# Layer 1's second MLP product with the weights moving and the tokens on the partitions, and the final norm along the rows

## The chip, the cores and the metric

The kernel runs on one core of a Trainium2 chip. The metric is the device time of one execution in microseconds, the median of several. Three runs of the kernel before gave 1903.33 us (1903.31 to 1904.78). TensorE (PE) multiplies into PSUM, VectorE (DVE) and ScalarE (ACT) read PSUM and work on SBUF, GpSimd (POOL) works on SBUF alone, and SyncE (SP) issues nearly all DMAs.

## What is computed

Two layers over 256 latent tokens and 256 context tokens, 1024 wide, in float32. After the attention-like branches each layer ends with the MLP below; layer 1's MLP and the final norm are for the latent tokens alone. The gate `g2` is a row of 1024 numbers, a sixth of `silu(c) @ w_ada[layer] + b_ada[layer]`.

```python
x = x + g1 * merge_branches(...)
x = x + g2 * squared_relu_mlp(modulate(rms_norm(x, norm2[layer]), sh2, sc2), w_up[layer], w_down[layer])
# squared_relu_mlp(h, w_up, w_down) = square(relu(h @ w_up)) @ w_down      w_up (1024, 4096), w_down (4096, 1024)
...
return rms_norm(x, final_norm)      # x * rsqrt(mean(x*x) + 1e-6) * final_norm
```

## The kernel before

**Layout.** `xT`, `hH`/`hL` and `yH`/`yL` are held transposed: features on the 128 partitions, tokens (context 0 to 255, latent 256 to 511) along the row, eight feature tiles `kt`. Each float32 operand is split in a high part (fp32r, written by ACT) and a rest (operand minus high part), and each product is made of three matmuls: high by high, high by rest, rest by high.

**Panels.** All large products are cut into 180 panels of 1024 x 256 weights, 1 MB each, numbered `p`. SP loads a panel into `raw[p % 4]` as soon as panel `p - 4` is done. ACT copies it to `wH[p % 3]` (`split`, two halves of 128x1024) and DVE subtracts into `wL[p % 4]`; ACT and DVE do this two panels ahead, at the beginning of their step for panel `p - 2`. PE (`run_panel`) holds a 128x128 tile of the weights and moves the tokens, 256 of them in layer 1 and 512 in layer 0, into `pp[p % 2]`, two banks per panel; the last matmul raises `panel_done`. Before its first matmul it waits for `slot_free[p % 2]` to reach `p // 2`: whoever reads the banks of a panel raises that semaphore afterwards. The order of all steps on all engines is the list `PLAN`, which `make_plan` writes out; each engine walks it and does its part of each step. `later` puts a step off until so many panels have been planned.

**The MLP.** Per quarter `g` of the 4096 hidden features four `up` panels and four `down` panels. After an `up` panel ACT takes relu into `y_tmp`, DVE squares, ACT writes `yH`, DVE `yL`. After a `down` panel DVE does two `scalar_tensor_tensor` (L1818), `xT += modT * pp`: so x is brought up to date in SBUF after every quarter. Layer 1 has 16 `down` panels, 152 to 155, 160 to 163, 168 to 171 and 176 to 179.

**Between `wo` and the MLP in layer 1.** `wo` (panels 144 to 147) updates `xT`; `squares` (ACT) and DVE sum x squared, `mean` (PE, L1058) adds across partitions, ACT takes the square root, DVE the reciprocal, `spread` (PE, L1068) spreads it along partitions, `apply` (DVE `n_t` and `n_h`, ACT `hH` L1482, POOL `hL`) makes the MLP's input. Around these stand `ada` steps (L1096): `c` times a piece of `w_ada`, four pieces for layer 1's `g2` (group 11). `adarow` (DVE) copies their sums to SBUF, `adaturn` (PE, L1123) turns them, `modulation` (DVE) adds `b_ada` and writes `modT`. The order is `ada ada squares mean ada spread ada apply`, then the first halves of two `up` panels.

**The end.** After each of the last `down` panels: `squares`, and `final_turn`, where ACT multiplies `xT` by `final_norm` into `f_x` and PE transposes it (L1079, four 128x128) into a `pc` bank. After the last panel: `final_mean` over the partitions, square root, reciprocal, and `final`: ACT scales the first 512 columns (L1455) and DVE the other 512 (L2133) from PSUM into `f_out`, and SP stores the two halves of the tokens (L945).

Of the kernel before, what the change touches and what calls it, by code (L numbers as in the profile page):

```python
# [180 lines left out]
def make_plan():  # L181
# [20 lines left out]
    def later(at, k, **kw):  # L202

        owed.append((at, lambda: step(k, 0, **kw)))
        owed.sort(key=lambda q: q[0])

    def row_turn(at, g):

        for wait, k in ((1, "adarow"), (2, "adaturn"), (2, "modulation")):
            later(at + wait, k, g=g)  # L210
# [48 lines left out]
    for l in range(DEPTH):  # L259
# [134 lines left out]
        spread_apply(l, 2, 1)  # L394
# [12 lines left out]
        step("squares", l + 1, n=1, j=NC - 1)  # L407
        if more:
            step("mean", l + 1, n=1)
            ada()  # L410
        else:
            step("final_mean", DEPTH, n=1)
            step("final_turn", DEPTH, n=1, j=NC - 1)
    step("final", DEPTH)
# [5 lines left out]
    group_use = {}  # L420
# [16 lines left out]
    for st in plan:  # L437
# [8 lines left out]
        elif k == "final_turn":  # L446

            if st["j"] % 2 == 0:
                for tt in range(LAT // P):
                    use(st, tt, 2 * (st["j"] // 2) + tt)  # L450
                turn_use = st["u"]
            else:
                st["u"] = turn_use
# [63 lines left out]
        elif k == "final":  # L517
            for j in (0, 2):
                q = next(q for q in plan if q["k"] == "final_turn" and q["j"] == j)
                for tt in range(LAT // P):  # L520
                    st["u"][j // 2, tt] = q["u"][tt]
# [11 lines left out]
def trunk(nc, x, c, ctx_in, c_ctx, w_ada, b_ada, norm1, norm2, w_in, gate_b, mnorm, qnorm, knorm, conv_w,  # L533
          w_pm, w_pa, w_pc, w_out, w_up, w_down, fnorm, consts, out):
    ctx = ExitStack()
    with ctx:
# [73 lines left out]
        f_x = at("f_x", [P, 2, LAT], F32, T + 30720)  # L610
# [7 lines left out]
        n_sd, n_rs = small[:, 4:8], small[:, 8:12]  # L618
        q_sd, q_rs = small[:, 16:24], small[:, 24:32]
        pars = [at(f"pars{i}", [P, P if i < 2 else 24], F32, o + 512 * i) for i in range(3)]; o += 1120  # L620
# [55 lines left out]
        fx_ready = sem("final_x_ready")  # L676
        fx_half = sem("final_x_first_tile")
        fa_ready = sem("final_first_half_ready")
        fx_used = sem("final_x_turned")
# [70 lines left out]

        def panel_source(st):
            kind, l, c, b = st["kind"], st["l"], st["c"], st["b"]
            if kind in COL:
# [35 lines left out]
        for st in PLAN:  # L789
# [14 lines left out]
            elif k == "panel" and st["kind"] in ("wo", "down"):  # L804
# [63 lines left out]
        def _(sp):  # L868
# [32 lines left out]
            def load_panel(p):  # L901
                sp.dma_start(raw[:, p % RAW, :, :], panel_source(PANELS[p])).then_inc(s_raw[p % RAW], 16)
# [4 lines left out]
            sp.dma_start(par_rows[2][16:24, :], fnorm.rearrange("(r q) -> r q", q=P)).then_inc(s_small, 16)  # L907
# [9 lines left out]
            for st in PLAN:  # L917
                if st["k"] == "panel" and (st["kind"], st["c"]) == ("mk", 0):
# [7 lines left out]
                    for g in range(2):  # L926
                        for dr in range(2):
                            sp.dma_start(gb[dr * 4:dr * 4 + 4, g:g + 1],
                                         gate_b[l, dr, g].rearrange("(h a) -> h a", a=1)).then_inc(s_wg, 16)
                if st["k"] == "pairload":  # L930
# [18 lines left out]
        def _(pe):  # L949
# [11 lines left out]

            def run_panel(st, kts=slice(0, KT)):
# [4 lines left out]
                hs_, ls_ = p % HIGH, p % RAW  # L967

# [49 lines left out]
            for st in PLAN:  # L1018
# [5 lines left out]
                elif k == "start":  # L1024
                    pe.wait_ge(s_small, 64)
                    filled(pe.transpose(claim(u["par2"])[:, 0:24], par_rows[2][0:24, :], ident[0:24, 0:24]), u["par2"])
# [19 lines left out]
                elif k in ("mean", "final_mean"):  # L1046

                    if k == "mean":
                        b = claim(u["ss"])
                    else:  # L1050
                        pe.wait_ge(slot_free[NPANELS % 2], NPANELS // 2)
                        b = pp[:, NPANELS % 2, 0, :]
# [6 lines left out]
                    if k == "mean":  # L1059
                        filled(last, u["ss"])  # L1060
                    else:
                        last.then_inc(panel_done, 1)
# [8 lines left out]
                elif k == "final_turn":  # L1071
                    j = st["j"]
                    pe.wait_ge(fx_half, j + 1)
                    pe.wait_ge(fx_ready, j + 1)
                    for tt in range(LAT // P):
                        b = claim(u[tt]) if j % 2 == 0 else pc[:, u[tt][0], :]
                        for i in range(2):
                            at_ = (j % 2 * 2 + i) * P
                            last = pe.transpose(b[:, at_:at_ + P], f_x[:, i, tt * P:(tt + 1) * P], ident)  # L1079
                        if j % 2:  # L1080
                            filled(last, u[tt])
                        elif tt:
                            last.then_inc(fx_used, 1)
# [204 lines left out]
        def _(act):  # L1288
# [25 lines left out]
            for st in PLAN:  # L1314
# [107 lines left out]
                elif k in ("mean", "final_mean"):  # L1422
# [4 lines left out]
                    if k == "mean":  # L1427
                        b = bank(act, u["ss"])
                    else:
                        act.wait_ge(panel_done, NPANELS + 1)  # L1430
                        b = pp[:, NPANELS % 2, 0, :]
                    act.activation(n_sd[:, t0:TT], b[:, t0:TT], ACT.Sqrt, bias=eps).then_inc(sd_ready, 1)
                elif k == "final_turn":

                    j = st["j"]
                    act.wait_ge(x_ready, x_needed(st))
                    if j:
                        if j % 2:
                            act.wait_ge(fx_used, j // 2 + 1)
                        else:  # L1440
                            for tt in range(LAT // P):
                                act.wait_ge(full[u0[tt][0]], u0[tt][1] + 1)
                    u0 = u
                    for i in range(2):
                        g = 16 + 2 * j + i
                        last = act.activation(f_x[:, i, :], xT[:, 2 * j + i, CTX:TOK], ACT.Copy, scale=pars[2][:, g:g + 1])
                        if i == 0:
                            last.then_inc(fx_half, 1)
                    last.then_inc(fx_ready, 1)
                elif k == "final":  # L1450

                    act.wait_ge(nrs_ready, n_norm)
                    for tt in range(LAT // P):
                        b = bank(act, u[0, tt])
                        act.activation(f_out[:, tt, 0:D // 2], b[:, :], ACT.Copy,  # L1455
                                       scale=n_rs[:, CTX // P + tt:CTX // P + tt + 1]).then_inc(fa_ready, 1)
# [218 lines left out]
        def _(dve):  # L1675
# [25 lines left out]
            for st in PLAN:  # L1701
                k, l, u = st["k"], st["l"], st["u"]
                if k == "start":
                    up = u["par2"]
                    freed(dve.tensor_copy(pars[2][:, :], bank(dve, up)[:, 0:24]), up)
# [35 lines left out]
                elif k == "panel":  # L1741
# [61 lines left out]
                    elif kind == "up":  # L1803
# [6 lines left out]
                                          ALU.subtract).then_inc(y_ready, 1)  # L1810
# [364 lines left out]
```

## Time and profile before

| | |
|---|---|
| median of 3 runs | 1903.33 us |
| the profiled execution | 1904.54 us |
| its span, first to last instruction | 1902.5 us |
| PE matmul busy | 1854.5 us (97%) |
| PE weight load busy | 1598.2 us (84%) |
| DVE, ACT, POOL busy | 1062.7, 690.4, 158.2 us |
| mean granted TensorE clock | 0.989 of full |
| DMA | 244.56 MB, mean 129 GB/s |

In a timeline a row gives the start, the time taken, the engine, the line of the kernel, the operation, output <- inputs, sizes and count; in brackets how long the engine had been idle and for whom. Consecutive matmuls overlap, so what one costs is the distance between two starts, not its own duration. A row of windows gives the stretch, its length, the busy time (and count) of PE, then, where asked for all engines, of PE weight loads, DVE, ACT and POOL, then the granted clock, the DMA share and GB/s. A row of groups gives line, engine, operation, operands, form, count, busy us and mean ns.

### The profile page before, as it was taken

What the parts mean: (1) busy time and instruction counts of PE and PEld (TensorE: products, weight loads), DVE (VectorE), ACT (ScalarE), POOL (GpSimd) and SP (SyncE); (2) the same over time, 40 slices, a digit from 0 to 9 for tenths busy, and PEclk for the clock granted to TensorE, in tenths of its full rate; (3) what the DMA queues carried; (4) which work ended last, traced back from release to release, by engine and by line L of the source; (5) the groups of instructions that cost most, each with busy time, mean ns of one, the idle gap of its engine ahead of it and who ended that gap; (6) DMA issues with size and microseconds to landing.
All of it is one profiled execution on the core that took longest, in us unless ns stands there. A gap on an engine that the chain in (4) does not pass through costs nothing.

```text
span 1902.5 us, 26175 instructions
## 1 busy us (share of the span) xinstructions
PE 1854.5 (97%) x10845; PEld 1598.2 (84%) x10845; DVE 1062.7 (56%) x1562; ACT 690.4 (36%) x946; POOL 158.2 (8%) x158
## 2 busy tenths in 40 slices
PE   6999999999999999989999999899999999999998
PEld 4797788888888888867888888699998899989997
DVE  5535643545556666467565554644646656566664
ACT  3423543333222222343232223333544434444443
POOL 2101100001110111220000000200100110120000
PEclk9999999999999999999999999999999999999999
DMA  9221122211443453624443525232242365555552
GB/s 322 69 87 45 45 89 67 67 61 51 133 147 119 151 191 101 221 95 149 133 136 130 199 89 180 66 110 70 65 132 89 111 222 181 190 184 180 188 187 89
DMA packets 226293, 244.56 MB, mean 129 GB/s; under 512 B 5796, under 2 KB 210944, under 8 KB 226176
## 3 DMA queue, kind: packets, MB, share of 16 engines
q1 hardware_dynamic: 225872, 242.80, 39.8%
q8 instruction: 86, 1.41, 0.3%
q14 instruction: 31, 0.25, 0.0%
q10 hardware_dynamic: 304, 0.10, 0.0%
HBM read 241.84 MB, written 1.05 MB: 128 GB/s over the span
## 4 chain that ended last, share of the span: by engine, by line
PE 91%; DVE 4%; ACT 1%; SPq 1%; issue 1%; DMA 1%; POOL 0%; DVEq 0%; ACTq 0%
PE pp L1004 20%; PE pp L1008 20%; PE pp L1005 19%; PE pp L1013 5%; PE pp L1011 5%; PE pp L1012 5%; PE pc L1193 3%; PE pp L986 2%; PE pp L987 2%; PE pp L988 2%; PE pc L1245 1%; PE pc L1283 1%; SPq L884 1%; PE pc L1260 1%; DMA raw<-in_w_in 1%
## 5 line engine op out<-in xcount | busy, mean ns | idle before, releaser
L1004 PE MATMUL pp<-hH,wH 128*128 128x512 f32 (+1 forms) x1760 | 590.9, 346 | 4.4 <-ACT hH L1482 4.4
L1005 PE MATMUL pp<-hH,wL 128*128 128x512 f32 (+1 forms) x1760 | 581.3, 341 | 0.0
L1697 DVE TENSOR_TENSOR wL<-raw,wH 128x1024 fp32r<-128x1024 f32 x358 | 448.6, 1294 | 203.3 <-ACT wH L1297 200.1
L1297 ACT ACTIVATE wH<-raw 128x1024 fp32r<-128x1024 f32 x360 | 360.4, 1050 | 356.1 <-PE pp L1013 173.9
L1008 PE MATMUL pp<-hL,wH 128*128 128x512 f32 (+1 forms) x1760 | 456.4, 341 | 2.6 <-POOL hL L1635 1.9
L1004 PEld LDWEIGHTS pp<-hH,wH 128*128 128x128 f32 x1760 | 335.2, 190 | 50.7 <-issue 14.8
L1005 PEld LDWEIGHTS pp<-hH,wL 128*128 128x128 f32 x1760 | 335.1, 190 | 37.6 <-issue 1.7
L1008 PEld LDWEIGHTS pp<-hL,wH 128*128 128x128 f32 x1760 | 304.3, 190 | 43.8 <-POOL hL L1635 6.8
L1011 PE MATMUL pp<-yH,wH 128*128 128x512 f32 (+1 forms) x448 | 150.8, 337 | 0.0
L1012 PE MATMUL pp<-yL,wH 128*128 128x512 f32 (+1 forms) x448 | 150.6, 336 | 0.0
L1013 PE MATMUL pp<-yH,wL 128*128 128x512 f32 (+1 forms) x448 | 150.6, 336 | 0.0
L1004 PE MATMUL pp<-yH,wH 128*128 128x512 f32 (+1 forms) x448 | 149.3, 344 | 0.0
L1005 PE MATMUL pp<-yH,wL 128*128 128x512 f32 (+1 forms) x448 | 146.0, 337 | 0.0
L1008 PE MATMUL pp<-yL,wH 128*128 128x512 f32 (+1 forms) x448 | 114.1, 336 | 0.0
L1818 DVE SCALAR_TENSOR_TENSOR xT<-pp,modT,xT 128x256 f32<-128x256 f32 x120 | 50.7, 478 | 98.9 <-PE pp L1013 98.8
L1870 DVE SCALAR_TENSOR_TENSOR acc<-pair_W,c_wide,acc 128x512 f32<-128x512 f32 x126 | 102.2, 848 | 3.8 <-DVE xT L1818 1.2
L1004 PEld LDWEIGHTS pp<-yH,wH 128*128 128x128 f32 x448 | 85.3, 190 | 10.9 <-issue 2.4
L1005 PEld LDWEIGHTS pp<-yH,wL 128*128 128x128 f32 x448 | 85.2, 190 | 9.4 <-issue 0.7
L1013 PEld LDWEIGHTS pp<-yH,wL 128*128 128x128 f32 x448 | 85.2, 190 | 8.7
L986 PE MATMUL pp<-wH,hH 128*128 128x256 f32 x320 | 92.5, 289 | 0.0
L1012 PEld LDWEIGHTS pp<-yL,wH 128*128 128x128 f32 x448 | 85.1, 190 | 8.7
L1011 PEld LDWEIGHTS pp<-yH,wH 128*128 128x128 f32 x448 | 85.1, 190 | 8.8
(235 smaller groups left out, 2076.6 us busy)
## 6 DMA issues: line engine op xcount, KB each, us to landing
raw<-in_w_in SPq DMA_DIRECT2D x84, 1024.0 KB, 5.2
raw<-in_w_up SPq DMA_DIRECT2D x32, 1024.0 KB, 5.6
raw<-in_w_down SPq DMA_DIRECT2D x32, 1024.0 KB, 5.2
pair_W<-in_w_ada SPq DMA_DIRECT2D x10, 2048.0 KB, 7.9
ada_Y<-in_w_ada SPq DMA_DIRECT2D x10, 1024.0 KB, 11.9
ada_H<-in_w_ada SPq DMA_DIRECT2D x8, 1024.0 KB, 11.9
raw<-in_w_proj_m SPq DMA_DIRECT2D x8, 1024.0 KB, 5.3
raw<-in_w_proj_a SPq DMA_DIRECT2D x8, 1024.0 KB, 5.4
```

Source lines behind the costliest of these rows:

```text
L986: pe.matmul(dst, hi[:, kt, ts_], wH[:, hs_, kt, :], start=kt == 0, stop=False)
L1004: pe.matmul(dsts[b], wh[b], hi[:, kt, ts_], start=first, stop=False)
L1005: pe.matmul(dsts[b], wl[b], hi[:, kt, ts_], start=False, stop=False)
L1008: last = pe.matmul(dsts[b], wh[b], lo[:, kt, ts_], start=False, stop=end)
L1011: pe.matmul(dsts[b], wh[b], hi[:, kt, ts_], start=first, stop=False)
L1012: pe.matmul(dsts[b], wh[b], lo[:, kt, ts_], start=False, stop=False)
L1013: last = pe.matmul(dsts[b], wl[b], hi[:, kt, ts_], start=False, stop=end)
L1193: last = pe.matmul(b[:, 0:MV + 1], EP[:, d, off:off + P], vaug[:, s, h, :], start=i == 0, stop=i == len(terms) - 1)
L1297: act.activation(wH[:, p % HIGH, a:a + KH, :], raw[:, p % RAW, a:a + KH, :], ACT.Copy).then_inc(wH_ready, 1)
L1697: dve.tensor_tensor(wL[:, p % RAW, ks, :], raw[:, p % RAW, ks, :], wH[:, p % HIGH, ks, :].bitcast(F32), ALU.subtract).then_inc(wL_ready, 1)
L1818: i = dve.scalar_tensor_tensor(out=xT[:, kt, hs], in0=pp[:, slot, b, hs], scalar=modT[:, l, g + kt, v:v + 1], in1=xT[:, kt, hs], op0=ALU.m ...
L1870: i = dve.scalar_tensor_tensor(out=acc[:, v, :], in0=src[:, kt, :], scalar=c2[:, kt, v:v + 1], in1=acc[:, v, :], op0=ALU.mult, op1=ALU.add)
```

## The change

- A `down` panel of layer 1 (`natural`) is now 512 rows by 512 columns of `w_down`: still 1 MB, column half `ch = c // 2`, row half `kh = c % 2`; `wide` views the same buffers as four tiles of 128x512. In `run_sums` PE holds a 128x128 tile of `yH` or `yL` (128 tokens) and moves 512 weight columns: 4 row tiles x 2 token halves x 3 = 24 matmuls a panel. They add into the four `pc` banks (column half x token half) from the first quarter to the last; `pp` is not used and x not updated between. The last panel of a column half (177 and 179) goes token half by token half.
- L1818 falls away for these 16 panels. In its place DVE waits for `panel_done` and raises `slot_free`, except after the last two panels. Panels 177 and 179 raise `full` of their banks and not `panel_done`.
- New `turn_nat`, twice: PE transposes eight 128x128 tiles of `xT` into two banks, ACT copies them to `x_nat` (two of 128x512). Once between `mean` and `spread`, in the place of an `ada`, which moves behind `spread`; once after the first `up` panel.
- New `gate_nat` in the place of `adaturn` and `modulation` of group 11: four 128x256 matmuls with float32 operands spread the gate row over all partitions in two banks; DVE adds `b_ada` (two of 128x512) into `g_nat`. SP loads `b_ada`'s row and `final_norm`, each repeated on 128 partitions, 512 KB each, ahead of panel 150.
- `squares`, `final_turn`, `final_mean` and `final` at the end are replaced by four `tail` steps (column half, token half), planned after panels 177 and 179.
- `final_norm` is no longer loaded by SP at the start (L907).

```diff
@@ make_plan
-        ada()
-        if l == 0:
+        if more:
+            ada()
+            spread_apply(l, 2, 1)
 ...
+        else:
+            step("turn_nat", l, half=0)
+            spread_apply(l, 2, 2)
+            later(count["panel"] + 1, "turn_nat", l, half=1)
 ...
-                if g == FF // D - 1 and c:
+                if more and g == FF // D - 1 and c:
                     step("squares", l + 1, n=1, j=c - 1)
-                    if not more:
-                        step("final_turn", DEPTH, n=1, j=c - 1)
+                if not more and g == FF // D - 1 and c % 2:
+                    for tt in range(LAT // P):
+                        step("tail", l, ch=c // 2, tt=tt)
@@ PE
+            def run_sums(st):
+                p, l, b_, u = st["p"], st["l"], st["b"], st["u"]
+                ch, kh = divmod(st["c"], 2)
+                first, end = (b_, kh) == (0, 0), (b_, kh) == (FF // D - 1, 1)
+                order = [(k_, tt) for k_ in range(KH) for tt in range(LAT // P)]
+                if end:
+                    order = [(k_, tt) for tt in range(LAT // P) for k_ in range(KH)]
+                for n, (k_, tt) in enumerate(order):
 ...
+                    pe.matmul(banks[tt], yH[:, kt, ts_], wh[:, k_, :], start=first and k_ == 0, stop=False)
+                    pe.matmul(banks[tt], yH[:, kt, ts_], wl[:, k_, :], start=False, stop=False)
+                    last = pe.matmul(banks[tt], yL[:, kt, ts_], wh[:, k_, :], start=False, stop=end and k_ == KH - 1)
+                    if end and k_ == KH - 1:
+                        filled(last, u[tt])
+                if not end:
+                    last.then_inc(panel_done, 1)
             def run_panel(st, kts=slice(0, KT)):
                 if p >= 2 and kts.start == 0:
                     pe.wait_ge(slot_free[slot], p // 2)
+                if natural(st):
+                    run_sums(st)
+                    return
@@ DVE
+                    elif natural(st):
+                        if p + 2 < NPANELS:
+                            dve.wait_ge(panel_done, p + 1)
+                            dve.sem_inc(slot_free[slot], 1)
+                elif k == "tail":
+                    if n == 0:
+                        dve.wait_ge(xn_ready, 2)
+                    dve.tensor_tensor(f_t[:, :], b, g_nat[:, cs], ALU.mult).then_inc(ft_ready, 1)
+                    dve.wait_ge(ft_ready, 2 * n + 1)
+                    v = x_nat[:, tt, cs]
+                    dve.tensor_tensor(v, v, f_t[:, :], ALU.add).then_inc(ft_ready, 1)
+                    dve.wait_ge(ft_ready, 2 * n + 2)
+                    i = dve.tensor_tensor(f_out[:, tt, cs], v, fn_nat[:, cs], ALU.mult)
+                    if ch == 0:
+                        i.then_inc(fn_ready, 1)
+                    else:
+                        start_link(i)
+                        dve.wait_ge(fd_ready, tt + 1)
+                        dve.reciprocal(n_rs[:, tt:tt + 1], n_sd[:, tt:tt + 1]).then_inc(fr_ready, 1)
+                        dve.wait_ge(dchain, count[0])
+                        dve.wait_ge(fr_ready, tt + 1)
+                        dve.tensor_scalar(f_out[:, tt, cs], f_out[:, tt, cs], n_rs[:, tt:tt + 1], None,
                                           ALU.mult).then_inc(f_ready, 1)
@@ ACT, tail
+                    act.wait_ge(ft_ready, 2 * n + 2)
+                    if n:
+                        act.wait_ge(fs_ready, n)
+                    act.activation(f_sq[:, :], x_nat[:, tt, ch * (D // 2):(ch + 1) * (D // 2)], ACT.Square,
+                                   accum_out=f_ss[:, n:n + 1]).then_inc(fs_ready, 1)
+                    act.wait_ge(fs_ready, n + 1)
+                    if ch == 0:
+                        act.activation(f_b[:, tt:tt + 1], f_ss[:, n:n + 1], ACT.Identity, scale=1.0 / D,
+                                       bias=eps).then_inc(fb_ready, 1)
                     else:
+                        act.wait_ge(fb_ready, tt + 1)
+                        act.activation(n_sd[:, tt:tt + 1], f_ss[:, n:n + 1], ACT.Sqrt, scale=1.0 / D,
+                                       bias=f_b[:, tt:tt + 1]).then_inc(fd_ready, 1)
+                        act.wait_ge(fr_ready, tt + 1)
+                        act.wait_ge(fn_ready, tt + 1)
+                        act.activation(f_out[:, tt, 0:D // 2], f_out[:, tt, 0:D // 2], ACT.Copy,
+                                       scale=n_rs[:, tt:tt + 1]).then_inc(fa_ready, 1)
```

## Rows read from the trace of the kernel before

**Rows 1.** Page, part 4: the chain that ended last, shares of the span.
```profile
PE 91%; DVE 4%; ACT 1%; SPq 1%; issue 1%; DMA 1%; POOL 0%; DVEq 0%; ACTq 0%
```

**Rows 2.** Windows, all engines: 50 us inside layer 1's MLP.
```profile
1750.00:1800.00 50.00, 50.00 (x419) 50.00 (x418) 29.35 (x36) 21.95 (x26) 0.00 (x0) 1.00 0.57 182
```

**Rows 3.** Timeline of PE: first matmul of panels 176 and 177, 256 columns moving.
```profile
1867.47 0.28 PE L1004 MATMUL pp<-yH,wH 128*128 128x256 f32 x1
...
1873.23 0.28 PE L1004 MATMUL pp<-yH,wH 128*128 128x256 f32 x1
```

**Rows 4.** Timeline of PE in layer 0's MLP, 512 columns moving, ten matmuls apart.
```profile
900.05 0.39 PE L1005 MATMUL pp<-yH,wL 128*128 128x512 f32 x1
...
902.32 0.39 PE L1005 MATMUL pp<-yH,wL 128*128 128x512 f32 x1
```

**Rows 5.** Windows, all engines: an `mv` panel, tokens held and weights moving.
```profile
1300.00:1304.00 4.00, 4.00 (x35) 4.00 (x35) 0.00 (x0) 0.00 (x0) 0.00 (x0) 1.00 0.00 0
```

**Rows 6.** Timeline of PE: `final_turn` between panels 177 and 178.
```profile
1878.99 0.60 PE L1079 MATMUL pc<-con,f_x 128*128 128x128 f32 x4
...
1879.55 0.28 PE L1005 MATMUL pp<-yH,wL 128*128 128x256 f32 x1
```

**Rows 7.** Timeline of PE from layer 1's second `mean` to the first `up` matmul.
```profile
1699.99 0.58 PE L1058 MATMUL pc<-small,n_sum 128*128 128x1 f32 x4 [1.32 <-DVE n_sum L1902]
1700.50 1.07 PE L1096 MATMUL pc<-ada_Y,c_wide 128*32 128x256 f32 x16
1701.50 0.86 PE L1068 MATMUL pc<-con,small 128*128 128x128 f32 x4
1702.29 1.94 PE L1096 MATMUL pc<-ada_Y,c_wide 128*32 128x256 f32 x16
1704.15 0.58 PE L1004 MATMUL pp<-hH,wH 128*128 128x256 f32 x1
```

**Rows 8.** Windows of PE alone: granted clock in that stretch.
```profile
1702.00:1703.00 1.00, 1.00 (x10) 0.50 0.00 0
```

**Rows 9.** Timeline of DVE and of ACT in that stretch.
```profile
1701.01 0.17 DVE L1908 RECIPROCAL small<-small 128x2 f32<-128x2 f32 x1 [1.17 <-ACT small L1432]
...
1702.98 1.32 ACT L1482 ACTIVATE hH<-n_t,modT,gain 128x256 fp32r<-128x256 f32 x2 [2.11 <-DVE n_t L1926]
```

**Rows 10.** Timeline of PE: `adaturn`, and four float32 products of 128x256 (eight records).
```profile
1717.17 0.61 PE L1123 MATMUL pc<-con,ada_rows 128*128 128x8 f32 x4 [0.27 <-DVE ada_rows L1728]
...
1444.68 1.89 PE L1283 MATMUL pc<-prT,v_a 128*128 128x256 f32 x8
```

**Rows 11.** Timeline, all engines, from the last panel's end.
```profile
1891.36 0.60 PE L1079 MATMUL pc<-con,f_x 128*128 128x128 f32 x4
...
1891.57 0.87 DVE L1818 SCALAR_TENSOR_TENSOR xT<-pp,modT,xT 128x256 f32<-128x256 f32 x2 [4.12 <-PE pp L1013]
...
1894.70 0.58 PE L1058 MATMUL pp<-small,n_sum 128*128 128x1 f32 x4 [2.74 <-DVE n_sum L1902]
...
1898.77 0.36 SPq L945 DMA_DIRECT2D out<-f_out  x1
```

**Rows 12.** Groups by form: the operations nearest to those of `tail`.
```profile
L1805 DVE TENSOR_TENSOR y_tmp<-y_tmp 128x512 f32<-128x512 f32 x16 | 11.1, 693 | 19.9 <-ACT y_tmp L1394 19.9
...
L2115 DVE TENSOR_SCALAR pr<-pr,ars 128x512 f32<-128x512 f32 x32 | 14.1, 483 | 0.7 <-DVE ars L2111 0.2
...
L1523 ACT ACTIVATION_READ_ACCUMULATOR junk<-hM 128x1 f32 x24 | 4.9, 203 | 0.0
L1527 ACT ACTIVATE mrs<-mss,small 128x2 f32<-128x2 f32 x4 | 1.2, 296 | 0.0
L1421 ACT ACTIVATE n_sq<-xT 128x512 f32<-128x512 f32 x6 | 3.7, 620 | 8.0 <-DVE xT L1818 8.0
L1455 ACT ACTIVATE f_out<-pc,small 128x512 f32<-128x512 f32 x2 | 1.3, 677 | 0.0
```

**Rows 13.** Timeline of SP's queue at the start.
```profile
1.96 0.29 SPq L907 DMA_DIRECT2D par_rows<-in_final_norm  x1
```

More of the change, by code:

```diff
@@ L406, in make_plan @@
             ada(2)
[L407 to L408 removed]
+            step("squares", l + 1, n=1, j=NC - 1)
             step("mean", l + 1, n=1)
             ada()
[L411 to L414, printed above, removed]
     assert count["ada"] == len(ADA) and not owed
@@ L445, in make_plan @@
             st["u"] = spread_use
-        elif k == "final_turn":
-            if st["j"] % 2 == 0:
+        elif k == "turn_nat":
+            for tt in range(LAT // P):
+                use(st, tt, 2 * tt)
+        elif k == "gate_nat":
+            for i in range(2):
+                use(st, i, 1 + 2 * i)
+        elif k == "panel" and st["kind"] == "down" and st["l"] == DEPTH - 1:
+            ch, kh = divmod(st["c"], 2)
+            if (st["b"], kh) == (0, 0):
                 for tt in range(LAT // P):
-                    use(st, tt, 2 * (st["j"] // 2) + tt)
-                turn_use = st["u"]
-            else:
-                st["u"] = turn_use
+                    use(st, tt, 2 * ch + tt)
+                sum_use[ch] = st["u"]
+            else:
+                st["u"] = sum_use[ch]
+        elif k == "tail":
+            st["u"] = {0: sum_use[st["ch"]][st["tt"]]}
         elif k == "turn_x":
@@ L803, in trunk @@
                 h_no[l, "m", st["j"]] = n_h_; n_h_ += 1
-            elif k == "panel" and st["kind"] in ("wo", "down"):
+            elif k == "panel" and st["kind"] in ("wo", "down") and not natural(st):
                 x_no[l, st["kind"], st["b"], st["c"]] = n_x; n_x += 1
@@ L1058, in _ @@
                         last = pe.matmul(b[:, tt:tt + 1], n_sum[:, tt * P:(tt + 1) * P], mean_d, start=True, stop=True)
[L1059 to L1062, printed above, removed]
+                    filled(last, u["ss"])
                 elif k == "spread":
@@ L1070, in _ @@
                     filled(last, u["rs"])
[L1071 to L1074, printed above, removed]
+                elif k == "turn_nat":
+                    half = st["half"]
+                    pe.wait_ge(x_ready, x_no[l, "wo", 0, 2 * half + 1] + 1)
                     for tt in range(LAT // P):
[L1076 to L1083, printed above, removed]
+                        b = claim(u[tt])
+                        for i in range(KH):
+                            last = pe.transpose(b[:, i * P:(i + 1) * P],
+                                                xT[:, half * KH + i, CTX + tt * P:CTX + (tt + 1) * P], ident)
+                        filled(last, u[tt])
+                elif k == "gate_nat":
+                    for i in range(2):
+                        b = claim(u[i])
+                        for c in range(2):
+                            r = 2 * (2 * i + c)
+                            last = pe.matmul(b[:, c * PC:(c + 1) * PC], row_sum[:, r:r + 1].to_broadcast([P, P]),
+                                             ada_rows[:, st["g"] % 2, :], start=True, stop=True)
+                        filled(last, u[i])
                 elif k == "ada":
@@ L1426, in _ @@
                         act.wait_ge(s_const, 4)
-                    if k == "mean":
-                        b = bank(act, u["ss"])
-                    else:
[L1430 to L1456, printed above, removed]
```

117 lines of the change are left out of this document (83 added, 34 removed).

## Prediction

> **What bounds the kernel now.** I read the chain of work that ended last first: 91% of the span is TensorE [rows 1]. Then windows of 50 us through layer 1's MLP: PE is busy in all 50, at full clock, DVE in 29.35 and ACT in 21.95, DMA at 0.57 [rows 2]. So in that stage time goes only with what PE issues; DVE, ACT and DMA work there is covered, and DVE's L1818, which the change removes 16 times, is worth nothing by itself. Then the two places where the MLP's neighbours set the time: from the second `mean` to the first `up` matmul [rows 7 to 9], and the end, from the last panel's end at 1891.36 to 1902.5, 11.1 us in which PE is nearly idle [rows 11]. The sum below is made on the profiled execution (1904.54, span 1902.5); the median of the runs is 1903.33, 1.2 lower, and I take the saving off the median.
>
> **1. The 16 panels: -5.1.** Panel 176 takes from 1867.47 to 1873.23, 5.76 us for 48 matmuls of 256 columns, 0.120 each [rows 3]. Ten matmuls of 512 columns take 2.27 us, 0.227 each [rows 4]. 24 of these are 5.44: 0.32 less per panel, 16 x 0.32 = 5.1. What goes is a part that each matmul costs however many columns it moves: 2 x 0.120 - 0.227 = 0.013. The bound from above is the same row. From below, the row of 512 has tokens moving and weights held, here it is the other way; the nearest row of that kind is the `mv` panel, 256 wide, 35 matmuls in 4 us, no slower than rows 3 [rows 5]. I keep 5.1, 4.6 at the least. The Trainium skill ("TensorE: Matmul & The Clock Gate", section Back-to-back issue gap) gives an issue gap of N/2.4 + 2.5 ns for a single stream. By that page 256 columns cost 0.109 and 512 cost 0.216, and the saving would be an estimated 16 x (48 x 0.1092 - 24 x 0.2158) = 1.0 us and not 5.1. Rows 3 and 4 disagree with it by 11 ns per matmul at both widths, and I go by the rows.
>
> Waits that could take the place: a `down` panel now needs only half of `yH` at first, so that is easier than before. Splits, loads (1 MB each as before) and the `slot_free` signals run two and more panels ahead, with 20 us of 50 free on DVE [rows 2]. None of it ends last, with one exception (part 4).
>
> **2. `final_turn` out of the panels: -0.9.** From the first of its four transposes to the second matmul of panel 178 are 0.56 us, and one matmul issue is 0.12: 0.44 [rows 6, 3]. Two of the four lie between panels: 0.9. The other two lie in the end, part 5.
>
> **3. Ahead of the MLP: +1.9.** (a) The `ada` between `mean` and `spread` took 1.00 (1700.50 to 1701.50) at full clock; eight transposes take its place, 0.09 each, 0.7 in all (a quarter of 0.44 less the slower first matmul) [rows 6, 7]. `spread` then starts when the reciprocal is there (1701.01 + 0.17), at 1701.25, 0.25 earlier, and with it `apply`. ACT's two copies (0.6 each, like L1421's 0.62) end near 1702.3 and `hH` is due at 1702.98 [rows 9, 12]: covered by 0.4, and if not, 0.4 is what it costs. But two `ada` stand behind `spread`, in the stretch where the clock is half (0.50) and one takes 1.86 (1702.29 to 1704.15) [rows 7, 8]. The first `up` matmul starts some 1.2 later than 1704.15. The matmuls it displaces would have run at half clock and behind `apply`, so most comes back; I take +0.2, between -0.2 and +1.2. (b) The second `turn_nat` has no idle time to go into: eight transposes, +0.7. Its two copies add 1.2 to ACT, covered by ACT's free half [rows 2]; without that cover, up to 1.2. (c) `adaturn` costs 0.27 of waiting and 0.46 of issue (0.61 less the 0.16 by which a matmul outlasts its issue). `gate_nat` is four float32 products of 128x256 in eight records, like L1283's, 1.89 - 0.16 = 1.73 [rows 10]. The wait is gone since PE comes 0.7 later: +1.0. The two adds on DVE (0.69 each, [rows 12]) have 20 us of 50 to go into. The two repeated rows, 1 MB, are issued by SP between panels 149 and 150, far ahead of use, at a DMA share of about 0.6: nothing. Sum 0.2 + 0.7 + 1.0 = 1.9, bounds +1.3 and +3.3.
>
> **4. A stall of PE ahead of the last panel: +0.4.** Panel 177 is the last of its banks and does not raise `panel_done`. DVE's step for it waits until `panel_done` is 178, which comes only when panel 178 is done, and only then raises `slot_free`, for which PE waits ahead of panel 179. The nearest row of such a hand-over is 0.21 from the last issue of PE to DVE's start (0.16 of it the matmul's own end) [rows 11]; back the same without the 0.16, with the semaphore step 0.4. Bounds 0.2 and 1.0. Queued behind that wait on DVE are the two `tail` steps of the first column half: meant to run beside panel 178, they begin when it ends.
>
> **5. The end, with the stall: -2.5.** Counted from the end of panel 178. Before: 0.44 + 5.76 + 11.13 = 17.3. After: DVE begins at 0.3 with tail 0 and 1, six operations of 0.69 and a hand-over of 0.05: to 4.75. The bank for tail 2 is full at 0.4 + 2.7 + 0.2 = 3.3, so DVE is late by 1.4. Tail 2: two operations to 6.2; ACT square 0.62, reading its sum 0.20, square root 0.30 with hand-overs to 7.4; reciprocal 0.2, scaling 0.48, to 8.1 [rows 12]. Tail 3's bank is full at 0.4 + 5.44 + 0.2 = 6.0, DVE comes at 8.1: 9.6, 10.8, reciprocal 11.0, ACT's 512 columns 0.68, 11.7. The last store before went from 1898.77 to the end at 1902.5, 3.7 [rows 11], beside the first one; alone on the DMA I count 3.1. 14.8 in all, 2.5 less. The bound from above is full overlap of all hand-overs and a store of 2.6, 3.4 less; from below 1.5 less. Of the 2.5 the stall of part 4 has already taken its 0.4.
>
> **6. The start: -0.2.** One DMA issue less on SP (0.29, from 1.96) ahead of the load of x, for which PE waits [rows 13]. 0 to 0.3.
>
> **Sum.** The last panel and the second `final_turn` lie inside part 5, so parts 1 and 2 count 15 panels (4.8) and one `final_turn` (0.4): -4.8 - 0.4 + 1.9 - 2.5 - 0.2 = **-6.0**. The profiled execution would go from 1904.5 to 1898.5 (span 1896.5), the median from 1903.3 to **1897.3**.
>
> **Rivals.**
> A. *The half clock comes more often.* The clock fell after an idle stretch of 1.32 us and the work at 1702 to 1705 ran at 0.50 [rows 7, 8]. The stall of part 4 and the new pauses could bring more such stretches: one like that from 1702 to 1705 costs half its length, 1.5, two cost 3.0. Against it: waits of 0.27 [rows 10] were followed by no fall. Two of them: 1903.3 - 6.0 + 3.0 = 1900.3.
> B. *The width gives nothing here*: with the weight buffers moving a matmul of 512 columns costs as much as two of 256, 0.240. Then 4.8 of the 6.0 are gone: 1902.1. Rows 4 speak against it, though with the roles the other way. By the rule of the Trainium skill's page cited in part 1 the gain of the width would be an estimated 1.0 and the time 1901.2.
> C. *The load of the held operand shows*, slower. PE now holds tokens and the weight load (busy like PE itself in rows 2) has to hide behind a matmul that reads rows of 512 from the weight buffers. If each of 384 matmuls cost 0.050 more (0.277), that is +19: 1916.5. It decides from 6.0/384 = 0.016 (a distance of 0.243) on, and is slower by over 0.2% from (6.0 + 3.8)/384 = 0.026 (0.253) on. Against it: rows 4, where PE's load hides, and rows 5, the same roles.
> D. *The tail goes better*: DVE's wait of part 4 does not bind and tails 0 and 1 run beside panel 178. Tail 2 then starts with its bank at 2.9 and takes DVE the same 3.35, tail 3 starts at 6.3 and not at 8.1: 1903.3 - 6.0 - 1.8 = 1895.5. The code speaks against it.
>
> **Chances.** Forecast 0.70, A 0.14, B 0.05, C 0.04, D 0.07. The ends of the terms, all at once, give savings from 4.3 + 0.4 - 3.3 + 1.5 = 2.9 (15/16 of 4.6, no gain at the start) to 4.8 + 0.4 - 1.3 + 3.4 + 0.3 = 7.6, so 1895.7 to 1900.4; to take in A and D the range is 1894.9 to 1900.8. B and C stay outside. What a measurement of this kernel can tell from no change is about 0.2%, 3.8 us. The forecast and D are faster by more than that; A (3.0) and B (1.2) are within it; C is slower. Faster 0.77, same 0.19, slower 0.04.
>
> **What would show it.** Right: matmuls of `run_sums` 0.227 apart and panels 5.44 apart; no idle time of PE inside the MLP but about 0.4 ahead of panel 179, put down to DVE; `gate_nat` 1.7; DVE busy without a gap from the end of panel 178 until tail 2's square root; about 9 us from PE's last matmul to the end. Wrong: a distance above 0.23, a clock under 1.00 in the MLP, PE waiting for `wL` or for DVE behind `gate_nat`, or the tails of the first column half beside panel 178.

## The result and the profile after

| | before | after |
|---|---|---|
| median | 1903.61 us (1903.31 to 1904.78, 4 runs) | 1891.97 us (1890.20 to 1894.92, 4 runs) |
| ratio | | 0.9939, 95% interval 0.9922 to 0.9957 |
| profiled execution | 1904.54 us | 1894.92 us |
| its span | 1902.5 us | 1893.2 us |

The saving is 11.6 us, where the forecast was 6.0 and the range ended at 1894.9. Run again beside other kernels (e5_change_again) the ratio was 0.9931. In e5_change_again one execution of six took 9583.39 us, and no trace shows why; it is in the median given for that run and not in its ratio. The profiled execution after is the slowest of its four, so its trace understates the saving (9.3 between the spans); the account below says by what.

Windows of all engines over 50 us of layer 1's MLP after, to be read against [rows 2]:

```profile
1750.00:1800.00 50.00, 50.00 (x333) 46.23 (x332) 26.79 (x26) 22.55 (x26) 0.00 (x0) 1.00 0.60 190
```

PE is still busy throughout at full clock; DVE has 26 operations in place of 36, and as forecast that is worth nothing by itself.

The timeline of PE at the end of panel 178 and the start of 179 (lines 1014 to 1016 are `run_sums`):

```profile
1878.07 0.39 PE L1016 MATMUL pc<-wH,yL 128*128 128x512 f32 x1
1878.30 0.39 PE L1014 MATMUL pc<-wH,yH 128*128 128x512 f32 x1
1878.53 0.39 PE L1015 MATMUL pc<-wL,yH 128*128 128x512 f32 x1
1878.75 0.39 PE L1016 MATMUL pc<-wH,yL 128*128 128x512 f32 x1
1879.26 0.50 PE L1014 MATMUL pc<-wH,yH 128*128 128x512 f32 x1
1879.59 0.39 PE L1015 MATMUL pc<-wL,yH 128*128 128x512 f32 x1
```

Starts are 0.227 apart, and 0.51 between the panels: the stall is 0.28. The next start is 0.33 later and not 0.227, and the panel's last matmul (1884.62) comes 0.43 later than it would have at 0.227 throughout.

Then the view I should have compared first, PE's longest waits. The columns are the waiting line, what ended the wait, total us, times, longest us. Before:

```profile
PE pc L1058 <- DVE n_sum L1902: 11.9, 4, 4.2
PE pc L1123 <- DVE ada_rows L1728: 5.1, 4, 3.4
```

After (L1118 is `mean`, L1186 `adaturn`):

```profile
PE pc L1118 <- DVE n_sum L1973: 11.9, 4, 4.3
PE pc L1186 <- DVE ada_rows L1795: 1.1, 2, 0.5
```

The second pair differs by 4.0 us, and only 0.27 of that is the wait of [rows 10]. One wait of 3.45 in layer 0 is nearly all the rest. Timeline of DVE and PE there, before:

```profile
855.62 1.23 DVE L1809 TENSOR_TENSOR yL<-y_tmp,yH 128x1024 fp32r<-128x1024 f32 x1 [1.13 <-ACT yH L1302]
...
856.76 0.88 DVE L1868 TENSOR_SCALAR acc<-pair_G,c_wide 128x512 f32<-128x512 f32 x2
...
857.68 2.86 DVE L1870 SCALAR_TENSOR_TENSOR acc<-pair_G,c_wide,acc 128x512 f32<-128x512 f32 x4
860.58 0.42 DVE L1728 COPY ada_rows<-pc 128x256 f32<-128x256 f32 x1
...
861.05 0.61 PE L1123 MATMUL pc<-con,ada_rows 128*128 128x8 f32 x4 [3.45 <-DVE ada_rows L1728]
```

After:

```profile
855.48 1.23 DVE L1876 TENSOR_TENSOR yL<-y_tmp,yH 128x1024 fp32r<-128x1024 f32 x1 [1.13 <-ACT yH L1365]
...
856.62 0.42 DVE L1795 COPY ada_rows<-pc 128x256 f32<-128x256 f32 x1
...
856.96 0.88 DVE L1939 TENSOR_SCALAR acc<-pair_G,c_wide 128x512 f32<-128x512 f32 x2
...
857.32 0.51 PE L1186 MATMUL pc<-con,ada_rows 128*128 128x8 f32 x4
```

The short copy for which PE waits now stands ahead of the six long operations of `weighted` and not behind them. The wait of 3.45 is gone. And so is what followed it. Windows with the granted clock as third number from the end, before and then after:

```profile
863.00:864.00 1.00, 1.00 (x3) 0.75 (x3) 1.00 (x2) 0.00 (x0) 0.00 (x0) 0.50 0.00 0
```

```profile
863.00:864.00 1.00, 1.00 (x6) 0.81 (x5) 1.00 (x2) 0.00 (x0) 0.00 (x0) 1.00 0.00 0
```

Why the order changed stands in the first hunk of the diff. In layer 0 `spread_apply(l, 2, 1)` used to come behind the block that queues the `weighted` steps with `later`; now it comes ahead of it. The `ada` inside it is the fourth piece of layer 0's own `g2`, so it queues `adarow` for the next panel. Both fall due at the same panel, the sort that takes them out keeps equals in the order in which they were queued, and so `adarow` now wins.

**An account by one row.** DVE's subtraction into `wL` of a given panel is the same work in both kernels, so its start is a clock that both traces share. Before, for panels 49, 97, 145, 154 and 178:

```profile
701.98 1.22 DVE L1697 TENSOR_TENSOR wL<-raw,wH 128x1024 fp32r<-128x1024 f32 x1
...
1267.28 1.22 DVE L1697 TENSOR_TENSOR wL<-raw,wH 128x1024 fp32r<-128x1024 f32 x1
...
1670.35 1.70 DVE L1697 TENSOR_TENSOR wL<-raw,wH 128x1024 fp32r<-128x1024 f32 x1 [4.91 <-ACT wH L1297]
...
1732.40 1.23 DVE L1697 TENSOR_TENSOR wL<-raw,wH 128x1024 fp32r<-128x1024 f32 x1 [0.25 <-ACT wH L1297]
...
1870.64 2.36 DVE L1697 TENSOR_TENSOR wL<-raw,wH 128x1024 fp32r<-128x1024 f32 x2 [0.25 <-ACT wH L1297]
```

After:

```profile
701.80 2.36 DVE L1764 TENSOR_TENSOR wL<-raw,wH 128x1024 fp32r<-128x1024 f32 x2
...
1261.92 1.23 DVE L1764 TENSOR_TENSOR wL<-raw,wH 128x1024 fp32r<-128x1024 f32 x1
...
1668.03 1.70 DVE L1764 TENSOR_TENSOR wL<-raw,wH 128x1024 fp32r<-128x1024 f32 x1 [4.91 <-ACT wH L1360]
...
1731.34 2.36 DVE L1764 TENSOR_TENSOR wL<-raw,wH 128x1024 fp32r<-128x1024 f32 x2 [0.26 <-ACT wH L1360]
...
1865.81 2.36 DVE L1764 TENSOR_TENSOR wL<-raw,wH 128x1024 fp32r<-128x1024 f32 x2 [0.26 <-ACT wH L1360]
```

| stretch | after less before | what it is |
|---|---|---|
| start to 701.98 | -0.18 | the start, and what varies from run to run there |
| to 1267.28 | -5.18 | the order in layer 0 |
| to 1670.35 | +3.04 | more work at half clock, no edit |
| to 1732.40 | +1.26 | ahead of and at the head of layer 1's MLP |
| to 1870.64 | -3.77 | 12 panels of 512 columns |
| to the span's end | -4.47 | 3 more such panels, a `final_turn`, the end |
| sum | -9.30 | 1902.5 to 1893.2 |

The third line is not the change's doing. Windows of PE alone, where both kernels do the same work, before and then after:

```profile
1292.00:1300.00 8.00, 8.00 (x56) 0.79 0.19 66
```

```profile
1286.00:1294.00 8.00, 8.00 (x43) 0.57 0.28 98
```

The half-clock stretch there is twice as long after (clock 0.57 against 0.79 of 8 us), and another one at 1429 likewise. In e5_change_again, the same kernel, that last place ran at full clock and the span was 1888.7. So single profiles of one kernel differ by several us in this way. The first stretch varies too: the row at 701.80 after stands at 700.12 in e5_change_again, so its -0.18 says nothing. The other stretches repeat: 560.12 after and 560.40 in e5_change_again for the second, 63.31 and 63.33 for the fourth, 134.47 and 134.46 for the fifth. With the third line taken out, the two traces differ by 12.3 us.

### The profile page after: what moved, and what is told of

It reads as the page before. It is cut to its first block, busy times and chain, and to the rows that moved or that the text cites. A ratio compares the mean times of both kernels' runs of the same rounds, so it can differ in the third digit from the quotient of the medians.

```text
span 1893.2 us, 25365 instructions
## 1 busy us (share of the span) xinstructions
PE 1851.3 (98%) x10461; PEld 1580.6 (83%) x10461; DVE 1052.4 (56%) x1537; ACT 691.0 (37%) x948; POOL 158.3 (8%) x158
## 4 chain that ended last, share of the span: by engine, by line
PE 91%; DVE 4%; SPq 1%; ACT 1%; issue 1%; DMA 1%; POOL 0%; DVEq 0%; ACTq 0%; POOLq 0%
PE pp L1068 19%; PE pp L1072 19%; PE pp L1069 19%; PE pp L1077 4%; PE pp L1076 4%; PE pp L1075 4%; PE pc L1256 3%; PE pp L1050 2%; PE pp L1051 2%; PE pp L1052 2%; PE pc L1308 2%; PE pc L1346 1%; PE pc L1016 1%; PE pc L1014 1%; PE pc L1015 1%; SPq L914 1%
## 5 line engine op out<-in xcount | busy, mean ns | idle before, releaser
L1068 PEld LDWEIGHTS pp<-hH,wH 128*128 128x128 f32 x1760 | 333.7, 190 | 47.6 <-issue 11.6
L1068 PE MATMUL pp<-yH,wH 128*128 128x512 f32 (+1 forms) x320 | 115.3, 367 | 0.0
L1075 PE MATMUL pp<-yH,wH 128*128 128x512 f32 (+1 forms) x320 | 114.3, 357 | 0.0
L1077 PE MATMUL pp<-yH,wL 128*128 128x512 f32 (+1 forms) x320 | 114.3, 357 | 0.0
L1076 PE MATMUL pp<-yL,wH 128*128 128x512 f32 (+1 forms) x320 | 114.3, 357 | 0.0
L1069 PE MATMUL pp<-yH,wL 128*128 128x512 f32 (+1 forms) x320 | 112.3, 358 | 0.0
L1051 PE MATMUL pp<-wL,hH 128*128 128x256 f32 x320 | 92.6, 290 | 0.0
L1052 PE MATMUL pp<-wH,hL 128*128 128x256 f32 x320 | 92.5, 289 | 0.0
L1072 PE MATMUL pp<-yL,wH 128*128 128x512 f32 (+1 forms) x320 | 88.4, 357 | 0.0
L1365 ACT ACTIVATE yH<-y_tmp 128x1024 fp32r<-128x1024 f32 (+1 forms) x48 | 40.6, 847 | 96.5 <-DVE y_tmp L1862 44.8
L1889 DVE SCALAR_TENSOR_TENSOR xT<-pp,modT,xT 128x256 f32<-128x256 f32 x88 | 36.7, 477 | 62.2 <-PE pp L1077 62.2
L1068 PEld LDWEIGHTS pp<-yH,wH 128*128 128x128 f32 x320 | 60.5, 189 | 10.9 <-issue 2.4
L1069 PEld LDWEIGHTS pp<-yH,wL 128*128 128x128 f32 x320 | 60.5, 189 | 9.3 <-issue 0.7
## 6 DMA issues: line engine op xcount, KB each, us to landing
ada_H<-in_w_ada SPq DMA_DIRECT2D x8, 1024.0 KB, 11.6
```

The costliest lines, as they stand in the source:

```text
L1051: pe.matmul(dst, hi[:, kt, ts_], wL[:, ls_, kt, :], start=False, stop=False)
L1052: last = pe.matmul(dst, lo[:, kt, ts_], wH[:, hs_, kt, :], start=False, stop=kt == KT - 1)
L1068: pe.matmul(dsts[b], wh[b], hi[:, kt, ts_], start=first, stop=False)
L1069: pe.matmul(dsts[b], wl[b], hi[:, kt, ts_], start=False, stop=False)
L1072: last = pe.matmul(dsts[b], wh[b], lo[:, kt, ts_], start=False, stop=end)
L1075: pe.matmul(dsts[b], wh[b], hi[:, kt, ts_], start=first, stop=False)
```

## The experiments

Each kernel was run beside the one before: 1904.31 us (9 runs) for the first four, 1905.21 (11) for the next two, 1904.97 (9) for the last two.

### The order in layer 0 alone, and the rest alone

Theory: the missing term is the order in layer 0, worth 5.1 or more. Rival: the terms that I did cost are larger than I said. e1_order is the kernel before with nothing but

```diff
         if l == 0:
+            spread_apply(l, 2, 1)
 ...
-        spread_apply(l, 2, 1)
+        else:
+            spread_apply(l, 2, 1)
```

and e2_old_order is the changed kernel with that call moved back behind the block of pairs.

```diff
-            spread_apply(l, 2, 1)
 ...  for i in range(NC): later(at + 31, "adaload", a=FILL_N1 + i)
+            spread_apply(l, 2, 1)
```

> The kernel before with one edit of the plan: in layer 0, spread_apply stands ahead of the list of weight pairs, as in the changed kernel. Theory (order): adarow, due with the same panel as the first weighted step, now comes first on DVE; PE's wait of 3.45 us for ada_rows near 860 us goes, and with it the half-clock stretch of 3.4 us that followed it (1.7 us): 5.1 us faster, about 1898.5, and no wait of PE for ada_rows over 1 us in the MLP of layer 0. Rival (sizes): the order is worth nothing and the panels, the end or the start were worth more than I said: about 1903.6, no change.

> The changed kernel with the old order of that place. Theory (order): the wait of 3.4 us comes back and the time goes from 1892.0 to about 1897, which is what was forecast for the change without this part (1897.3). Rival (sizes): it stays at 1892.

Measured: e1_order 1898.53 (1897.22 to 1900.58, 5 runs), ratio 0.9967 (0.9955 to 0.998), so -5.8. e2_old_order 1897.73 (1895.7 to 1899.24, 5 runs), ratio 0.9961 (0.9947 to 0.9975), so -6.6. Together -12.4. In e2_old_order the wait is back in PE's waits:

```profile
PE pc L1186 <- DVE ada_rows L1795: 4.5, 3, 3.4
```

and the clock behind it is down again (windows, all engines):

```profile
863.00:864.00 1.00, 1.00 (x3) 0.75 (x3) 1.00 (x1) 0.00 (x0) 0.00 (x0) 0.50 0.04 13
```

In e1_order the wait and the half clock are gone from that place:

```profile
PE pc L1125 <- DVE ada_rows L1730: 1.6, 3, 0.8
```

```profile
862.00:863.00 1.00, 1.00 (x6) 0.84 (x5) 0.74 (x1) 0.23 (x1) 0.00 (x0) 1.00 0.00 0
```

The account by one row says the same without the scatter of whole runs. Panels 49 and 97 in e1_order:

```profile
700.27 2.36 DVE L1699 TENSOR_TENSOR wL<-raw,wH 128x1024 fp32r<-128x1024 f32 x2
...
1260.40 2.36 DVE L1699 TENSOR_TENSOR wL<-raw,wH 128x1024 fp32r<-128x1024 f32 x2
```

That is 560.13, as after (560.12), against 565.30 before: 5.17 less, from this edit alone. With the old order in the changed kernel (e2_old_order) it is 564.39; its low stretch at 1203 is half as long as the 6.8 us of the other two.

So the order alone is worth 5.8 us (3.8 to 8.6 by its interval), and everything that the prediction did cost is worth 6.6 (4.8 to 10.1 by its interval), beside a forecast of 6.0.

### The width of the matmul

e4_half_width: the changed kernel with each product of `run_sums` but the very first of a bank cut in two of 256 columns.

```diff
-                    pe.matmul(banks[tt], yH[:, kt, ts_], wh[:, k_, :], ...)
+                    cuts = [(0, 2 * PC)] if first and k_ == 0 else [(0, PC), (PC, 2 * PC)]
+                    for y_, w_, i_ in ((yH, wh, 0), (yH, wl, 1), (yL, wh, 2)):
+                        for a_, e_ in cuts:
+                            last = pe.matmul(banks[tt][:, a_:e_], y_[:, kt, ts_], w_[:, k_, a_:e_], ...)
```

> The changed kernel with each matmul of the 16 panels cut into two of 256 columns with the same held tokens, all else the same (the first product of each bank stays whole). Theory (a fixed part per matmul): start to start 0.120 us, panels 5.76 instead of 5.44, 16 x 0.32 = 5.1 us slower than the changed kernel, about 1897. Rival (the gain is in what else changed, the width gives nothing; or a fixed part of 2.5 ns only): 0 to 1.0 us slower, at most 1893.

Measured: 1896.71 (1894.92 to 1899.46, 4 runs), ratio 0.9959 (0.9946 to 0.9973). Against the change's 0.9939 and 0.9931 that is 4 to 5 us more. The intervals touch, and the trace is clearer: from `wL` of panel 154 to that of 178, 12 of these panels, it takes 138.12 (1727.04 to 1865.16), against 134.47 after and 138.24 before. So 3.65 of the 3.77 come back. The same 50 us of its MLP:

```profile
1750.00:1800.00 50.00, 50.00 (x419) 50.00 (x418) 25.48 (x26) 21.16 (x25) 0.00 (x0) 1.00 0.58 183
```

and its matmuls in pairs, each pair 0.24 after the last:

```profile
1789.99 0.40 PE L1017 MATMUL pc<-wH,yH 128*128 128x256 f32 x2
1790.23 0.40 PE L1017 MATMUL pc<-wL,yH 128*128 128x256 f32 x2
```

419 matmuls, exactly as many as before [rows 2], against 333 wide and narrow ones after. So a matmul costs 0.120 at 256 columns and 0.227 at 512, whichever operand is held, and the 13 ns that go with each matmul are what the width buys. By the figure of the Trainium skill's page "TensorE: Matmul & The Clock Gate" (Back-to-back issue gap), N/2.4 + 2.5 ns, which the section gives for a matmul in isolation, the width would have been worth an estimated 1.0 us; this run does not agree.

### The stall ahead of the last panel

e3_no_stall: the changed kernel, where PE does not wait for the banks `pp` ahead of panel 179 (it doesn't use them) and DVE skips its own wait in the step of panel 177.

```diff
-                if p >= 2 and kts.start == 0:
+                if p >= 2 and kts.start == 0 and p < NPANELS - 1:
 ...
-                        if p + 2 < NPANELS:
+                        if p + 3 < NPANELS:
```

> The changed kernel; PE does not wait for slot_free ahead of the last panel, and DVE does not wait for panel_done in its step for panel 177 (the last panels don't use pp). Theory (stall and late tails): PE's pause of about 0.3 us ahead of panel 179 goes, tails 0 and 1 run beside panel 178, tail 3 starts some 1.7 us sooner: 2.0 us faster, about 1890.0, tail 0 starting about 5.4 us before panel 179 does. Rival (the end is bound by tail 3 alone, or by the stores): only the 0.3 us of the pause, 1891.7.

Measured: 1890.02 (1889.16 to 1893.2, 5 runs), ratio 0.9925 (0.9912 to 0.9937); again, as e8_no_stall_again, 1889.98 (1887.85 to 1891.77, 4 runs), ratio 0.9919 (0.9905 to 0.9933). The intervals overlap with the change's, so times alone don't settle it; the trace does. Timeline of DVE, the first rows of tail 0 and tail 2:

```profile
1868.53 0.68 DVE L2215 TENSOR_TENSOR f_t<-pc,g_nat 128x512 f32<-128x512 f32 x1
...
1878.70 0.69 DVE L2215 TENSOR_TENSOR f_t<-pc,g_nat 128x512 f32<-128x512 f32 x1 [5.98 <-PE pc L1016]
```

Tail 0 now begins beside the second half of panel 177 (panel 178 starts at 1870.34), 7.25 ahead of panel 179's start at 1875.78, where I had expected 5.4; tail 1 follows at 1870.59, and tail 2 waits only for its own bank. From `wL` of panel 178 (here 1862.61) to the end of the span (1888.4) there are 25.8 us, and after 27.4 (1865.81 to 1893.2): 1.6 less. e8_no_stall_again gives 25.8 too (1862.73 to 1888.5), and e5_change_again 27.4 as after. So the stall's own 0.28 is the small part; the larger one is the tails queued behind DVE's wait. By its medians this is the fastest kernel of the study, if by little.

> The kernel of e3_no_stall again, beside e7_ada_in_the_gap on one chip. Every theory: ratio to before 0.9925 as earlier, about 1890.0 us.

### Where the turn stands

The change itself once more, as the yardstick for the next kernel:

> The changed kernel as it is, run again beside the next kernel so that both are timed on one chip. Every theory: 1892.0 us, the same ratio to before as earlier (0.9939), since nothing is altered. Beyond 0.2% from that, comparisons between calls are not worth more than their own before runs.

Measured: 1891.59 us, ratio 0.9931 (0.9918 to 0.9944).

e6_turns_early is e3_no_stall with the turn moved to where PE is idle:

```diff
         step("squares", l, n=2, j=NC - 1)
+        if not more:
+            step("turn_nat", l, half=0)
         step("mean", l, n=2)
 ...
-            step("turn_nat", l, half=0)
+            step("turn_nat", l, half=1)
             spread_apply(l, 2, 2)
-            later(count["panel"] + 1, "turn_nat", l, half=1)
```

> The changed kernel with two edits: the wait of the last panel is left out as in e3_no_stall, and layer 1's final-norm turn is moved to where TensorE stands idle: half 0 ahead of the mean (idle there 1.3 us while the squares come), half 1 between the mean and the spread, and nothing of it behind the first panel of the up product. Theory 1, the middle costs what TensorE issues there beside no other work: half 0's 8 transposes of 0.11 us (about 0.9 us) move into the idle stretch, so 0.7 to 0.9 us less than e3_no_stall's 1890.0, hence about 1889.2. Rival, what the path needs there is ScalarE, which evicts the turned rows and then takes the root of the mean: the copies stand in front of it, the turn shows again, and the time is 1890.0 or up to 1 us above it.

Measured: 1891.07 (1888.97 to 1892.59, 5 runs), ratio 0.9925 (0.9914 to 0.9937). No gain over e3_no_stall, and the rival held. It named ScalarE, and its timeline shows why; after:

```profile
1695.88 1.28 ACT L1491 ACT_TABLE_LOAD   x1
...
1698.29 0.26 ACT L1491 ACTIVATE small<-pc,small 128x2 f32<-128x2 f32 x1 [1.12 <-PE pc L1118]
```

and in e6_turns_early:

```profile
1693.89 1.08 ACT L1499 ACTIVATE x_nat<-pc 128x512 f32<-128x512 f32 x2 [1.18 <-PE pc L1136]
1695.08 1.28 ACT L1492 ACT_TABLE_LOAD   x1
1696.37 0.26 ACT L1492 ACTIVATE small<-pc,small 128x2 f32<-128x2 f32 x1
```

After, the table load lies in the idle time ahead of the mean (1697.68). Here the two copies stand in front of it, and the root comes 1.24 later against the mean. Dropping the turn behind the first `up` panel gives some of it back: from `wL` of panel 145 to that of 178 there are 197.8 us after (1668.03 to 1865.81), 197.8 in e3_no_stall (1664.83 to 1862.61) and 198.7 here (1664.88 to 1863.56).

e7_ada_in_the_gap avoids that: half 0 of the turn behind `wo`'s third panel, an `ada`, which needs nothing of ACT, in the idle stretch.

```diff
+            if not more and c == 2:
+                step("turn_nat", l, half=0)
         settle()
-        ada(2)
+        ada(2 if more else 3)
 ...
-            step("turn_nat", l, half=0)
-            spread_apply(l, 2, 2)
-            later(count["panel"] + 1, "turn_nat", l, half=1)
+            step("turn_nat", l, half=1)
+            spread_apply(l, 2, 1)
```

> The changed kernel without the wait of the last panel (as e3_no_stall), and layer 1's middle in another order: the final-norm turn's half 0 (features whose x is final two panels earlier) behind wo's third panel, three ada steps instead of two ahead of the mean, half 1 between mean and spread, one ada behind spread, nothing behind the first up panel. TensorE issues the same in all. Theory: what failed in e6_turns_early was ScalarE (copies ahead of its table load, root 1.2 us later), not the filling of TensorE's idle stretch; an ada needs nothing of ScalarE. So the root comes as early as in e3_no_stall, about 1.0 of the 1.3 us idle ahead of the mean is filled, and the time is 1.0 us below e3_no_stall in the same call. Rival: something else of the middle is what ends last there (the chain from the last wo panel through squares, mean, root, spread, apply to the first up product), and the time stays at e3_no_stall's.

Measured: 1890.96 (1888.55 to 1893.75, 5 runs), ratio 0.992 (0.9907 to 0.9934), beside e8_no_stall_again's 0.9919: not the 1.0 us less of my theory. The theory fell and the rival held. Timeline of PE:

```profile
1698.40 0.58 PE L1119 MATMUL pc<-small,n_sum 128*128 128x1 f32 x4 [0.45 <-DVE n_sum L1974]
...
1701.78 0.35 PE L1069 MATMUL pp<-hH,wH 128*128 128x256 f32 x1 [0.37 <-ACT hH L1550]
...
1704.88 0.51 PE L1073 MATMUL pp<-hL,wH 128*128 128x256 f32 x2 [0.36 <-POOL hL L1703]
...
1715.24 1.99 PE L1145 MATMUL pc<-ada_rows,con 128*128 128x256 f32 x8 [0.27 <-DVE ada_rows L1796]
```

The idle time ahead of the mean did fall from 1.31 to 0.45. But the mean came no earlier: it starts 30.50 behind `wL` of panel 145 and not 29.64 as in e8_no_stall_again, since half 0 of the turn now stands behind a panel where PE has no idle time. What that half no longer costs behind the first `up` panel came back only in part, for PE now waits for `hH`, `hL` and `ada_rows`, of which e8_no_stall_again shows only the one for `hL`. From `wL` of panel 145 to that of 178 it is 198.3 us (1667.90 to 1866.22), 0.55 more than e8_no_stall_again's 197.8 (1664.96 to 1862.73). In this middle PE follows a chain on other engines: mean, root, `spread`, `apply` on DVE, ACT and POOL. The `ada` steps around `spread` are cover for that chain, and fewer of them make nothing earlier. That fits the traces of after, e3_no_stall, e6_turns_early and e7_ada_in_the_gap; whether the chain alone accounts for the 0.55 was not tried by itself.

## Why the prediction was wrong

**The step that failed** is the list of parts itself. The prediction costs the change in six parts, and layer 0 is in none, though the first hunk of the diff moves a line there. I took the `if more:` for a regrouping with the same plan behind it. The order edit was worth 5.2 us in the trace (3.45 of waiting, 1.7 for 3.4 us at half clock) and 5.8 by itself as a kernel; with it the sum would have been -11.1, and 1892.2 beside the measured 1892.0. That this comes so close is luck in part: items 3 and 5 below were each 0.6 off, both the same way. The signs were there: PE's waits give 5.1 us over four waits for `ada_rows`, of which I quoted only one of 0.27 [rows 10]. And the half-clock stretch at 863 lies directly behind the longest.

**The other steps.**

1. *Panels, -5.1.* Right. Starts 0.227 apart, 12 panels worth 3.77 in the account (0.314 each, forecast 0.32), and e4_half_width gives 3.65 of them back.
2. *`final_turn`, -0.9.* Right. From `wL` of panel 178 to the end of panel 178 there are 13.17 us after and 14.54 before; less three panels at 0.314 that leaves 0.43 for the one outside the end, forecast at 0.4.
3. *Ahead of the MLP, +1.9.* Too high: +1.26. In (a) I counted PE's instructions, and not the chain on the other engines that PE waits for there. `n_t` starts 2.12 behind `mean` (1697.68 to 1699.80) and not 2.48 (1699.99 to 1702.47), and the first `up` matmul follows 3.80 behind `mean` (1701.48) and not 4.16 [rows 7]: -0.36, below my bound of -0.2. Some 0.15 of that isn't the change's doing but the clock's: e1_order has the old middle and no fall of the clock there, its `n_t` starts 2.33 behind `mean`, and from panel 145 to 154 it takes 61.90 against 62.05 before and 63.31 after. The eight transposes cost 0.79 (1711.20 to 1711.99). `gate_nat` took 1.53 (1714.94 to 1716.47) and not 1.73, which is 1.07 more than `adaturn`'s 0.46. The wait that `adaturn` leaves was larger than its 0.27: the matmul before it started at 1716.62 and it at 1717.17, 0.55 for a distance of 0.12, so 0.43 went; the 0.27 is counted from that matmul's end and not from its issue. -0.36 + 0.79 - 0.43 + 1.07 is 1.07. The other 0.2 lies in the first matmul behind each new group, whose successor starts 0.20 later where it was 0.12, and 0.31 where it was 0.21.
4. *The stall, +0.4.* There, in the place named and by the mechanism named: 0.28 between the panels, 0.43 at the last matmul of panel 179.
5. *The end, -2.5.* 14.2 from the end of panel 178 and not 14.8, so -3.1. Timeline of DVE after:

```profile
1879.37 0.69 DVE L2215 TENSOR_TENSOR f_t<-pc,g_nat 128x512 f32<-128x512 f32 x1 [7.55 <-PE pc L1016]
...
1886.00 0.16 DVE L2226 RECIPROCAL small<-small 128x1 f32<-128x1 f32 x1 [0.39 <-ACT small L1518]
...
1889.21 0.16 DVE L2226 RECIPROCAL small<-small 128x1 f32<-128x1 f32 x1 [0.39 <-ACT small L1518]
```

   Counted from 1878.98, the end of panel 178, tail 0 begins at 0.4 (forecast 0.3), tail 2's reciprocal at 7.0 (forecast about 7.4) and tail 3's at 10.2 (forecast about 10.8). Each hand-over was a little cheaper than I took it: DVE's operations follow at 0.72 and, from tail to tail, at 0.61, and ACT's chain from the end of the sum (1884.89) to the reciprocal takes 1.1 where I had 1.2.
6. *The start, -0.2.* The first transpose of x does start 0.20 earlier (7.18 against 7.38). That the row of panel 49 moved by 0.18 is luck: it stands at 701.80 and 700.12 in two profiles of the changed kernel, and at 700.27 in e1_order, which has the old start.

Items 1 to 6 as measured: -0.18 + 1.26 - 3.77 - 4.47 = -7.2 in the trace (-7.0 without the start) and -6.6 by e2_old_order, for a forecast of -6.0: inside the range I had for them.

**The rivals.** A (half clock more often) didn't happen at the stall; the clock stayed at full through panel 179. But its reason, that the clock fell at 1702 after 1.32 us of idle time, doesn't hold up: e1_order, after and e5_change_again have 1.31 ahead of the same `mean` and full clock behind it. Such stretches do make profiles of one kernel differ: of the 4.5 us between after and e5_change_again, 1.7 lie ahead of panel 49 and 3.1 between panels 97 and 145. B (the width gives nothing) and C (the held operand's load shows) fell with the 0.227. D (the first tails beside panel 178) isn't what the change does, but e3_no_stall made it so: 1.6 less, where D had 1.8.

## What to carry to other kernels

Before costing a diff, line up what each engine issues in both kernels, in order, and look for everything that moved, also in stages that the change isn't about; a line moved across a queue with stable order moves work. Read the waits of the bounding engine in full, with totals, and for each part of the change ask which of them it touches. A short copy that another engine waits for belongs ahead of long work that nobody waits for, and such a wait costs more than its length where the clock falls behind it. Idle time of TensorE ahead of a reduction is worth filling only if the chain behind it isn't what ends last.

## What the runs showed of the hardware that I had not expected

- Between a wait of 3.45 us and the fall of the granted clock to 0.50 (1.2 GHz) there was about 1 us of normal work, and the low stretch then lasted 3.4 us: the wait cost 5.2 and not 3.45. The two traces that have this wait (before and e2_old_order) show the low stretch, and the eight without it stayed at full clock there.
- Low stretches of 3.4 and 6.8 us (at the start of after one of 10.2) come at the same places, and the same kernel has the longer or the shorter from run to run: e5_change_again and the profiled run of after differ by 4.5 us in span (1888.7 and 1893.2), but from `wL` of panel 178 to the end both take 27.4 us (1861.30 to 1888.7, 1865.81 to 1893.2).
- The part of a matmul that doesn't depend on its width was 13 ns with weights held and with tokens held alike (0.120 at 256 columns, 0.227 at 512).
